# Second feed-forward stage of a two-block layer: down projections of pairs of feature tiles as seven block products, three of seven weight casts on ScalarE

## What is computed

```python
gate = h @ w_ffn_gate      # (1024 tokens, 2816)
val  = h @ w_ffn_up        # (1024 tokens, 2816)
y    = (silu(gate) * val) @ w_ffn_down   # (1024 tokens, 1024)
out  = x + modulated_rmsnorm(y)
```

## Time and profile before

| | |
|---|---|
| median of 3 runs | 2813.68 us (2813.31 to 2816.59) |
| profiled execution | 2818.23 us, span 2816.4 us |
| TensorE busy | 2724.6 us, 97% of the span, 13138 matmuls |
| GpSimd busy | 1596.1 us, 57% |
| VectorE busy | 1659.5 us, 59% |
| ScalarE busy | 849.7 us, 30% |
| mean granted TensorE clock | 0.992 of full speed |

### The profile page before, as it was taken

The page is one execution under the profiler, slowest core; times in us unless marked ns, Lnnn a source line. Parts: engine busy times, 40 slices in busy tenths (PEclk is TensorE's granted clock), DMA queues, the critical chain, the costliest instruction groups (busy, mean ns, idle before and its releaser), DMA issues.

```text
span 2816.4 us, 38237 instructions
## 1 busy us (share of the span) xinstructions
PE 2724.6 (97%) x13138; PEld 2180.7 (77%) x13138; DVE 1659.5 (59%) x2364; ACT 849.7 (30%) x1675; POOL 1596.1 (57%) x1242
## 2 busy tenths in 40 slices
PE   8999999898999999999999999989999999999998
PEld 5777777686878888887788887767777878888887
DVE  6666687738467777777834303484445446556556
ACT  5544444435211111114322114554233100100112
POOL 4566311455987777765523243212366987777764
PEclk9999999999999999999999999999999999999999
DMA  4322321044111111124411342213424121111134
GB/s 145 102 83 90 98 83 53 16 142 168 38 45 60 52 45 61 50 89 153 180 45 50 85 149 94 83 53 109 163 91 157 33 65 45 60 52 45 60 127 142
DMA packets 76809, 243.75 MB, mean 87 GB/s; under 512 B 7151, under 2 KB 11024, under 8 KB 76308
## 3 DMA queue, kind: packets, MB, share of 16 engines
q1 hardware_dynamic: 54608, 184.31, 20.1%
q10 hardware_dynamic: 22084, 57.86, 5.8%
HBM read 207.00 MB, written 32.52 MB: 85 GB/s over the span
## 4 chain that ended last, share of the span: by engine, by line
PE 81%; DVE 9%; POOL 5%; ACT 3%; issue 2%; DMA 0%; POOLq 0%; ACTq 0%; DVEq 0%; SPq 0%
PE ps L825 16%; PE ps L827 16%; PE ps L826 16%; PE ps L1150 7%; PE ps L1151 7%; PE ps L1152 7%; PE ps L916 2%; PE ps L932 2%; POOL arena L715 1%; PE ps L1433 1%; PE ps L1445 1%; PE ps L947 1%; DVE ps L2521 1%; DVE ps L2538 1%; DVE ps L2562 1%
## 5 line engine op out<-in xcount | busy, mean ns | idle before, releaser
L647 POOL CAST wh<-raw 128x1024 fp32r<-128x1024 f32 x175 | 186.4, 1065 | 843.2 <-PE ps L827 787.3
L825 PE MATMUL ps<-hh,wh 128*128 128x512 f32 x1456 | 598.9, 411 | 15.9 <-DVE hl L2481 11.3
L827 PE MATMUL ps<-hh,wl 128*128 128x512 f32 x1456 | 571.5, 393 | 0.0
L826 PE MATMUL ps<-hl,wh 128*128 128x512 f32 x1456 | 570.2, 392 | 0.0
L649 POOL TENSOR_TENSOR wl<-raw,wh 128x1024 fp32r<-128x1024 f32 x175 | 422.8, 2416 | 14.0
L741 POOL TENSOR_TENSOR wl<-raw,wh 128x512 fp32r<-128x512 f32 x256 | 344.4, 1345 | 20.5
L825 PEld LDWEIGHTS ps<-hh,wh 128*128 128x128 f32 x1456 | 275.1, 189 | 87.8 <-issue 15.5
L827 PEld LDWEIGHTS ps<-hh,wl 128*128 128x128 f32 x1456 | 274.5, 189 | 59.9
L826 PEld LDWEIGHTS ps<-hl,wh 128*128 128x128 f32 x1456 | 275.6, 189 | 52.1 <-issue 3.3
L825 PE MATMUL ps<-gated,wh 128*128 128x512 f32 (+1 forms) x728 | 279.7, 384 | 3.5 <-DVE gated L2572 3.2
L826 PE MATMUL ps<-gated,wh 128*128 128x512 f32 (+1 forms) x728 | 278.4, 382 | 0.0
(11 more groups left out here) (345 smaller groups left out, 5082.9 us busy)
## 6 DMA issues: line engine op xcount, KB each, us to landing
raw<-weights SPq DMA_DIRECT2D x271, 512.0 KB, 3.5
arena<-w_ada SPq DMA_DIRECT2D x48, 512.0 KB, 3.8
arena<-gate_scratch ACTq DMA_DIRECT2D x20, 512.0 KB, 5.1
arena<-x_t ACTq DMA_DIRECT2D x1, 4096.0 KB, 14.2
x_scratch<-arena ACTq DMA_DIRECT2D x2, 2048.0 KB, 9.1
arena<-x_scratch SPq DMA_DIRECT2D x2, 2048.0 KB, 10.1
gate_scratch<-arena ACTq DMA_DIRECT2D x16, 256.0 KB, 2.1
x_scratch<-arena ACTq DMA_DIRECT2D x1, 4096.0 KB, 13.8
```

Of the source, the lines that this page charges most:

```text
L647: pool.tensor_copy(wh[:, s], raw[:, r]).then_inc(Z.wt_hi, 1)
L825: pe.matmul(out, wh[:, slot, w], xh, start=start, stop=False)
L826: pe.matmul(out, wh[:, slot, w], xl, start=False, stop=False)
L827: return pe.matmul(out, wl[:, slot, w], xh, start=False, stop=stop)
```

## The change

1. **Pairs.** Feature tiles 4 to 19 form eight pairs. The down projections of a pair are now seven block products as well: the two tiles are the halves of the inner dimension, 2 x 512 output features and 2 x 512 tokens the others. A block product is 4 outputs x 3 = 12 matmuls, 84 for a pair in place of 96.
2. **Units.** The work is a row of units of two chunks (512 KB each) and seven block products: up projections of the first tile, down projections of the pair before, up projections of the second tile. Unit 1 is the up projection of tile 5, unit 22 that of tile 19, unit 23 the down projection of the last pair, which stands after the four half tiles. Tile 4 stays as it was.
3. **Weights.** Of a unit's seven blocks three need no sum. Their casts are made by ScalarE (`cast`), their low parts by GpSimd (`direct_low`). GpSimd has 4 casts, 7 low parts and 4 sums in each unit. `pair_load` loads the first chunk of a unit after part 5 of the unit before, the second after part 6.
4. **Activations.** VectorE and ScalarE make the block sums of the pair's products and their high and low parts (`first_blocks`, `second_blocks`), and VectorE makes 28 additions for a pair's down projections in place of 32.
5. **The end.** Tile 19's down projections leave `half_down` and `last_quarters`; unit 23 takes their place once.

The diff, cut to its core (k is the unit's number, ks the same as a constant for choosing buffers):

```diff
+        PAIRS = ST_N // 2
+        PAIR_LOOPS = (PAIRS - 1) // 2
+        C_PAIR, CT2 = C_ST[1], tail_at(C_FFN2)
+        LAST_UP, LAST_DOWN = 3 * PAIRS - 2, 3 * PAIRS - 1
...
+        UP_DIRECT, DOWN_DIRECT = (0, 2, 6), (0, 1, 6)
...
+        D_MOVING = [(A12_H, A12_L), (A11_H, A11_L), (S2_H, S2_L), (S3_H, S3_L), (A22_H, A22_L), (S1_H, S1_L), (S4_H, S4_L)]
+        D_LOWS = {0: 8, 2: 10, 6: 11}
+        D_FRESH = (0, 1, 5)
+        D_OUT = ((0, 0), (0, 0), (4, 0), (4, 1), (0, 1), (4, 1), (4, 0))
...
+        def slot_user(k, ks, i):
+            if ks == LAST_DOWN and i < 6:
+                return Z.chunk_done, CT2 + 2 + i // 2
+            if i == 6:
+                return R.unit_done, up_done(k, 0)
+            if ks == 1:
+                return R.unit_done, unit_done(1, 0, min(i + 3, 7))
+            return R.unit_done, up_done(k, i + 1) - ST_BLOCKS
...
+            def pair_load(k, ks, part):
+                c, r = (k - ks) * 2 + pair_chunk(ks, part), pair_chunk(ks, part) % RAW
+                sp.wait_ge(R.unit_split, unit_split(1, 0, (6, 8)[part]) if ks == 1 else up_split(k, 5 + part) - ST_BLOCKS)
+                sp.dma_start(raw[:, r], A.w[c] if isinstance(c, int) else A.w[bass.ds(c, 1)].rearrange("a p n -> p (a n)")).then_inc(
+                    (Z.raw0, Z.raw1)[r], 16)
...
+                sp.wait_ge(R.unit_split, up_split(LAST_UP, 5))
+                tail_load(0)
+                sp.wait_ge(R.unit_done, up_done(LAST_UP, 6))
+                for i in range(2):
+                    sp.dma_start(A21[1][i], A21_DRAM[i]).then_inc(R.a21_in, 16)
+                sp.wait_ge(R.unit_split, up_split(LAST_UP, 6))
+                tail_load(1)
+                for n in range(2, 6):
+                    weights(CT2 + n)
+                for n in range(2):
+                    sp.wait_ge(R.unit_split, up_split(LAST_DOWN, 5 + n))
+                    tail_load(6 + n)
+                    if n == 0:
+                        dram, x = x_half(1, 0)
+                        sp.dma_start(x, dram).then_inc(R.x_back0, 16)
...
+                def direct_low(i, j, src):
+                    w, slot = up_slot(ks, i)
+                    pool.wait_ge(R.w_cast, direct_cast(k, j))
+                    pool.sem_inc(Z.pace, 1)
+                    pool.tensor_tensor(wl[:, slot, w], src, wh[:, slot, w].bitcast(F32), ALU.subtract).then_inc(R.unit_split, 1)
+                def part(i, src, ready, count):
+                    w, slot = up_slot(ks, i)
+                    pool.wait_ge(R.unit_hi, ops + ready)
+                    pool.wait_ge(*slot_user(k, ks, i))
+                    pool.sem_inc(Z.pace, 1)
+                    pool.tensor_copy(wh[:, slot, w], src).then_inc(R.unit_hi, 1)
+                    pool.wait_ge(R.unit_hi, ops + count)
+                    pool.tensor_tensor(wl[:, slot, w], src, wh[:, slot, w].bitcast(F32), ALU.subtract).then_inc(R.unit_split, 1)
+                def weight_sub(dst, p, q):
+                    pool.tensor_tensor(dst, p, q, ALU.subtract).then_inc(R.unit_hi, 1)
+                def second_chunk():
+                    pool.wait_ge(*pair_loaded(k, ks, 1))
+                    pool.sem_inc(Z.pace, 1)
+                if down:
+                    direct_low(0, 0, b21)
+                    direct_low(1, 1, b11)
+                    second_chunk()
+                    pool.wait_ge(R.unit_split, up_split(k, 1))
+                    weight_sub(b11, b12, b11)
+                    pool.wait_ge(R.unit_hi, ops + 1)
+                    weight_sub(weight_sum[:], b22, b11)
+                    part(2, weight_sum[:], 2, 3)
+                    weight_sub(b12, b22, b12)
+                    part(3, b12, 4, 5)
+                    pool.wait_ge(R.unit_split, up_split(k, 0))
+                    weight_sub(b21, b21, weight_sum[:])
+                    part(4, b21, 6, 7)
+                    part(5, b11, 7, 8)
+                else:
+                    direct_low(0, 0, b11)
+                    second_chunk()
+                    pool.wait_ge(R.unit_split, up_split(k, 0))
+                    weight_sub(b11, b12, b11)
+                    pool.wait_ge(R.unit_hi, ops + 1)
+                    weight_sub(b12, b22, b12)
+                    part(1, b12, 2, 3)
+                    direct_low(2, 1, b21)
+                    weight_sub(weight_sum[:], b22, b11)
+                    part(3, weight_sum[:], 4, 5)
+                    pool.wait_ge(R.unit_split, up_split(k, 2))
+                    weight_sub(b21, b21, weight_sum[:])
+                    part(4, b11, 6, 7)
+                    part(5, b21, 7, 8)
+                direct_low(6, 2, b22)
...
+                def pair_down(pair, k, ks):
+                    for u in range(ST_BLOCKS):
+                        w, slot = up_slot(ks, u)
+                        xh, xl = D_MOVING[u]
+                        if u in D_LOWS:
+                            pe.wait_ge(Z.a_lo, lows(pair, D_LOWS[u]))
+                        pe.wait_ge(R.unit_split, up_split(k, u))
+                        for f in range(4):
+                            t = slice(w.start + f * P, w.start + (f + 1) * P)
+                            pe.wait_ge(Z.dn_free, pair * PAIR_SUMS + (DN_FIRST + 4 * u + f + 1))
+                            pe.matmul(bank(4 + f), wh[:, slot, t], xh, start=u in D_FRESH, stop=False, skip_group_check=True)
+                            pe.matmul(bank(4 + f), wh[:, slot, t], xl, start=False, stop=False, skip_group_check=True)
+                            last = pe.matmul(bank(4 + f), wl[:, slot, t], xh, start=False, stop=True, skip_group_check=True)
+                            last.then_inc(R.unit_done if f == 3 else Z.dn_done, 1)
...
+                    pair_up(0, 1, 1, 1)
+                    pair_up(1, 0, 2, 2)
+                    pair_down(0, 3, 3)
+                    pair_up(1, 1, 4, 4)
+                    with pe.Fori(0, PAIR_LOOPS) as i:
                         for u in range(2):
-                            c = i * 6 + ffn_gate(c0, 2 + u)
-                            up(i * 2 + (2 + u), c)
-                            down(i * 2 + (1 + u), 1 - u, c + 2, down_slot)
+                            m, k = i * 2 + (2 + u), i * 6 + (5 + 3 * u)
+                            pair_up(m, 0, k, 5 + 3 * u)
+                            pair_down(i * 2 + (1 + u), i * 6 + (6 + 3 * u), 6 + 3 * u)
+                            pair_up(m, 1, i * 6 + (7 + 3 * u), 7 + 3 * u)
...
                 low, high = range(4), range(4, KT)
-                half_down(0, 0, range(KT))
+                if use:
+                    pair_down(PAIRS - 1, LAST_DOWN, LAST_DOWN)
+                    pe.sem_inc(Z.chunk_done, 2)
+                else:
+                    half_down(0, 0, range(KT))
...
+            def cast(k, ks, down, j):
+                i = (DOWN_DIRECT if down else UP_DIRECT)[j]
+                (b11, b21), (b12, b22) = pair_raw(ks, 0), pair_raw(ks, 1)
+                src = ((b21, b11, b22) if down else (b11, b21, b22))[j]
+                w, slot = up_slot(ks, i)
+                pace(*slot_user(k, ks, i))
+                pace(*pair_loaded(k, ks, 1 if j == 2 else 0))
+                act.activation(wh[:, slot, w], src, ACT.Copy).then_inc(R.w_cast, 1)
...
+            def first_up(m, prev, k, ks):
+                second_highs(prev, lambda: pair_copy(m * 2, k))
+                cast(k, ks, False, 2)
+                last_high2(prev)
+                cast(k + 1, ks + 1, True, 0)
+                silu_first(m * 2, k)
+                cast(k + 1, ks + 1, True, 1)
+                silu_second(m * 2)
+            def down_casts(k, ks):
+                cast(k, ks, True, 2)
+                cast(k + 1, ks + 1, False, 0)
+                cast(k + 1, ks + 1, False, 1)
+            def second_up(m, k, ks, more=True):
+                first_highs(m, lambda: pair_copy(m * 2 + 1, k))
+                cast(k, ks, False, 2)
+                if more:
+                    cast(k + 1, ks + 1, False, 0)
+                silu_first(m * 2 + 1, k)
+                if more:
+                    cast(k + 1, ks + 1, False, 1)
+                silu_second(m * 2 + 1)
...
+            def first_blocks(pair, k):
+                n = pair * 2
+                value_sum(n, k)
+                gate_half(n, 1)
+                gate_half(n, 0)
+                dve.wait_ge(Z.f_prod, n * 2 + (ST_DONE + 2))
+                dve.wait_ge(Z.a_hi, highs(pair, 2))
+                block_sum(S3_F, 2, G1_F, ALU.subtract)
+                block_low(pair, 2, A11_L, bank(2), A11_H)
+                block_low(pair, 3, S3_L, S3_F, S3_H)
+            def second_blocks(pair, k):
+                n = pair * 2 + 1
+                gate_half(n, 1)
+                value_sum(n, k)
+                gate_half(n, 0)
+                dve.wait_ge(Z.a_hi, highs(pair, 4))
+                block_sum(S1_F, 3, G1_F, ALU.add)
+                dve.wait_ge(Z.a_lo, lows(pair, 3))
+                block_sum(S2_F, 3, S3_F, ALU.subtract)
```

(16 more changed lines are left out.)

361 lines of the change are left out of this document (281 added, 80 removed).

## The result

| | before | changed |
|---|---|---|
| median | 2815.05 us (2813.31 to 2816.59, 4 runs) | 2855.35 us (2849.55 to 2856.13, 4 runs) |
| ratio | | 1.0139, 95% interval 1.0121 to 1.0156 |
| profiled execution | 2818.23 us, span 2816.4 | 2855.09 us, span 2853.3 |
| mean granted TensorE clock | 0.992 | 0.987 |

The account below looks back on a forecast made before the run. GpSimd's circle with its reload, 20.9 us a unit against TensorE's 19.04, was taken as the bound; +16.6 to unit 22's end, +24.1 in the end and -4.3 in the quarters gave +36.4, 2850 us (2826 to 2870).

Parts of the forecast that it names:

- The saving of TensorE: Down projections: 72 matmuls of 512 columns fewer, 16.3 us, and 48 of 256 columns fewer, 5.8 us.
- The circle: Each unit: GpSimd's list to part 5's low part 16.4 us, load 3.79, ScalarE's cast 0.60, handover 0.15; 20.9 us in all.
- The turn: Between units: from part 5's low part to the next low part 0, through load, ScalarE's cast and handover; 4.5 us.
- The conflict: Units 2 to 22: 28 VectorE operations with two SBUF inputs slow GpSimd by 0.45 us each, 12.6 us.
- Unit 22: End of the last up unit: its circle begins at 2716.3, TensorE ends it at 2738.9, +16.6 us over before.
- The end: After unit 22: more matmuls, pauses, slow clock and a wait for VectorE, +24.1 us; fewer matmuls in the quarters, -4.3.
- (a): Rival for the units: TensorE stays the bound because loads and casts turn round fast enough; 2803.6 us, chance 0.07.
- (b): Rival for the units, the even case: the turn is 2.8 us; 2808 to 2819 us, chance 0.05.
- (c): Rival: no conflict of VectorE and GpSimd, 2838 us; with the pause behind h's transfers hidden too, 2829; chance 0.20.
- (e): Rival: ScalarE's ordered list joins the circle, each unit's cast 0 0.6 us late, 12.6 more; 2863 us, chance 0.12.
- (f): Rival: the change doesn't do what it says, ScalarE casting only when GpSimd is done; given no chance of its own.
- (d): Rival, whole lock: GpSimd stands still for all of each of 28 VectorE operations, 0.37 us more each; 2860 us, chance 0.13.

Follow-up runs that it names:

- e7: Change with the edits of e1 and e2 together (raw buffers freed earlier, h's transfers behind the loads): 2797.32 us, ratio to before 0.9934.
- e1: Change with GpSimd's sums stored elsewhere and part 4 or 5 made last, so both raw buffers are free earlier: 2806.97 us, ratio to before 0.9973.
- e9: Change with VectorE's low parts of block sums S1 to S4 cut to two columns and left out of the result: 2843.16 us.
- e5: Change with 29 more VectorE subtractions in units 2 to 22, both inputs in SBUF, ahead of the block sums' low parts: 2859.00 us.
- e4: Change with the three casts of each unit's direct blocks moved back from ScalarE to GpSimd: 2871.39 us.
- e2: Change with the two transfers of h issued after the loads for the first four half tiles: 2843.93 us.

## Why the prediction was right

**The saving of TensorE.** Predicted 22.1 us, less 1.5 of cover in the quarters: 20.6. In e7, where nothing waits for weights, the stretch is 18.1 us shorter than before. The 1.5 us of cover weren't lost, as shown below for the end, so 4.0 us are missing: 2.8 in the units, and 1.1 in one wait for VectorE's first addition of unit 23. TensorE as the bound: the forecast had 22 x 19.04 = 418.9 us for the units; e1 needs 2693.88 + 0.23 - 2272.43 = 421.7. The 2.8 us are in "16 take 10.89 us, 0.68 each, as long as three matmuls". VectorE's additions of a down unit in e7 are one row:

```profile
2424.70 19.41 DVE L3627 TENSOR_TENSOR hlf<-ps,hlf 128x512 f32<-128x512 f32 x28 [2.70 <-PE ps L1464]
```

That is 0.693 each where three matmuls take 0.680, and in that unit TensorE's groups of three start 0.70 apart (2439.72, 2440.42, 2441.12, ...), with no wait shown. Each of the seven down units of e7 takes 19.40 us from start to start, where an up unit takes 19.06; that is 2.5 of the 2.8 us:

```profile
2439.72 0.40 PE L1462 MATMUL ps<-sums,wh 128*128 128x512 f32 x1
...
2440.42 0.39 PE L1462 MATMUL ps<-sums,wh 128*128 128x512 f32 x1
```

That VectorE paces TensorE there is read from these rows, and wasn't tested.

**The circle.** Predicted 20.93 us with no conflict, counted from 1.37 us ahead of unit 1's sums, since these wait for their chunk. Without the conflict (e9) the sums are this row:

```profile
2259.98 2.67 POOL L925 TENSOR_TENSOR raw<-raw 128x512 f32<-128x512 f32 x2 [1.93 <-DMA raw<-weights]
```

From 2258.61 to low part 0 of unit 22 at 2702.52 are 443.9 us or 21.14 each, 4.4 more than the sum had for 21 circles. GpSimd's idle time for the second chunk, ahead of line 925, sums to 3.4 us: its load, issued 1.25 us behind the first, was late in up units, and I had only asked whether the first chunk would be in time. The turn is 4.62 us in the mean where the sum had 4.54, another 1.7 us. With these two nothing is left over.

**The conflict.** This is the term that was mis-sized: "I take 0.45 each", 12.6 us, measured 7 to 9, 0.27 to 0.31 each. Half of what one 1024-wide operation cost GpSimd was too much for a mean. None of the operations fell into a gap: in the change GpSimd has 29 operations that are longer than alone, as many as VectorE has such low parts, by 0.16 to 0.48 us each. Only the longest of them cost the 0.45 that I had taken for all.

**Unit 22.** Predicted: its low part 0 at 2716.3, TensorE's end at 2738.9, +16.6. Measured: 2716.12, and 2739.09 + 0.23 = 2739.3, +17.0 over the earlier trace rows. It agrees to 0.4 us because two errors nearly cancel: in the same count the change takes 451.5 us (from 2264.6, where I had 2264.2), so 7.6 for the conflict in place of 12.6, and the circle is 4.4 longer. The sum is better than its terms.

**The end.** Predicted +24.1 - 4.3 = +19.8. Measured: 2853.3 - 2739.3 = 114.0 us against 2816.4 - 2722.3 = 94.1, so +19.9. Here too two errors cancel. Divided at the first matmul of the second group that reads `mats` (2764.65 before, 2807.33 in the change), the first part is 25.7 us longer, not 24.1, and the quarters are 5.8 shorter, not 4.3. In the quarters nothing was lost for the cover: the wait of 1.48 us in the earlier trace rows is 0.86 here, with one of 0.28 later. In the first part: first pause 1.1, measured 0.70; pause behind the transfers 6.6, measured 7.90; slow matmuls 1.6, measured 1.4; the first addition 1.2, measured 1.29. That is 0.8 of the 1.6 us; the rest is spread over pieces of a few tenths.

The 6.6 was short by one step, "GpSimd could start 8.45 us after that load was issued": from 2740.48 it took 9.72 us, to 2750.20. The load 0.55 us behind it (line 661 above) isn't the reason, since before had one at the same distance from 2712.60:

```profile
2713.15 0.65 SPq L578 DMA_DIRECT2D raw<-weights  x1
```

The step took 9.16 us in the second profile of the change (2734.92 to 2744.08) and 8.83 in e1 (2695.41 to 2704.24), with the same transfers in the same order. So a part of it is what executions differ by; why isn't known.

**The rivals.** (a) and (b), TensorE the bound or nearly, needed turns of at most 2.6 and 2.8 us; it was 4.60. e1 shows that (a) would have been right had the buffer been released earlier: 2806.97 us measured, 2803.6 priced. (c), no conflict, falls with e9 and e5. (e), ScalarE's list, falls with e4. (f) falls with the group of line 2683. (d) needs a sentence more. I had priced the whole lock at 0.82 us for an operation, half of the 1.63 for which VectorE's was shown. But part of what is shown is VectorE's own waiting: in e9 its operations of two columns take 148 ns at least but 490 in the mean, and GpSimd's operations beside them have the mean of those alone, 1.29 us:

```profile
L3569 DVE TENSOR_TENSOR sums<-sums_f,sums 128x2 fp32r<-128x2 f32 x29 | 13.7, 490 | 4.4 <-ACT sums L2691 4.4
```

In the change the 28 take 1253 ns in the mean where 692 is the shortest, so VectorE loses 0.56 on each and GpSimd 0.31. Each engine waiting while the other has its turn would look like this. So the rule that the prediction drew on, of the Trainium skill, SBUF — State Buffer, section "SBUF: two separate sides", that the two exclude each other for a whole instruction, isn't refuted by these runs. What failed was the price that I hung on it: GpSimd can lose at most what VectorE's operation takes once it has begun, 0.69 us, and not what it is shown with.

**Chances and range.** 0.43 for the forecast case; the stretch came out within 0.1 us of the sum, the two medians at +35.3 and +40.3 over their own before. That is closer than the terms deserve: in the loop and in the end errors of 1.5 to 5 us cancel, and that is luck.

## What to carry to other kernels

An engine that is busy for 58% can be the bound, if its buffer is reloaded only at the end of its list: add up the list to the release, the load, and every handover behind it, and compare that circle with the engine that should set the pace. The cure here was to release the buffer earlier (e1: 44 us, from where three sums are stored and which part comes last) and taking work from the list alone (e4 against the change: 18 us) left it the bound. And ask for each transfer that stands ahead of an urgent one on its queue when it is really needed (e2: 10 us). When operations of two engines are longer side by side, read from each engine's own rows what it loses: a part of a long duration is that engine's own waiting, and not what the other one loses.

## What the runs showed of the hardware

- VectorE's subtraction of 512 columns took 0.68 us with an input in PSUM, always, and 0.68 to 1.78 us with both in SBUF, where GpSimd works beside it. Two columns took 0.15 us at least and 0.49 in the mean.
- A reload of 512 KB took 3.79 us from the last reader to the next; 256 KB took 0.93 less.
- TensorE's clock fell behind some short pauses and not behind others. From 2270 to 2740 us the change has 12 gaps of 1.8 to 2.4 us between starts; behind five of them, 1.1 to 1.6 us after TensorE went on, seven or eight matmuls start 0.43 us apart, the lower level of the clock (granted 0.50 from 2357.3 to 2360.6), and then full pace is back. In the change's second timing the same twelve gaps had one such group behind them, in e2 two. Before, and in e1 up to the end of unit 22, there are no such gaps and no slow matmuls. It explains the 0.97 of the window shown. It cost next to nothing: with five groups the stretch is 579.6 us and with one 578.7, since TensorE waits for the circle anyway. What decides it isn't known from these runs. Rows of the first group:

```profile
2356.06 0.50 PE L1410 MATMUL ps<-gated,wh 128*128 128x512 f32 x1 [1.79 <-POOL wl L922]
...
2357.32 0.63 PE L1412 MATMUL ps<-gated,wl 128*128 128x512 f32 x1
2357.75 0.63 PE L1410 MATMUL ps<-gated,wh 128*128 128x512 f32 x1
...
2360.73 0.40 PE L1411 MATMUL ps<-al,wh 128*128 128x512 f32 x1
```

- The start of unit 1 moved by 5 us between executions in which nothing ahead of it differed; comparisons of a few microseconds are better made from a mark in the trace than from the end.
